# Running the mixer front in four groups of 1, 2, 3 and 2 blocks instead of three of 1, 3 and 4, beside the expert retrieval

## The reference, cut to what matters

```
n  = rmsnorm(x) * (1 + sc1) + sh1
z  = n @ w_in                          # 1024 x 4096, split in a_lin, a_gate, u, v, g_a, g_b
a  = a_lin * sigmoid(a_gate)
a  = silu(layernorm(causal_dwconv(hist ++ a, width 31))) @ w_conv_out     # branch A
v  = layernorm(v)
b  = (u * (tril(w_s) @ v + b_s)) @ w_gmlp_out                             # branch B, chunks of 128
m  = sigmoid(g_a) * a + sigmoid(g_b) * b
x  = x + gt1 * (m @ w_out)
n2 = rmsnorm(x) * (1 + sc2) + sh2
q  = n2 @ w_q;  s1, s2 = q halves @ keys; top 16 of each; top 16 of their 16 x 16 sums -> 128 experts a token
act = gelu(u_tab[eid] . n2);  x = x + gt2 * sum(softmax * act * v_tab[eid])
y  = rmsnorm(x)
```

## Time and profile before

| | us |
|---|---|
| median of three runs | 3551.34 (3548.37 to 3553.54) |
| the profiled execution | 3556.78 |
| its span | 3555.2 |
| first gather | 275.3 |
| first gather of block 1 | 923.5 |
| first gather of block 4 | 2154.6 |
| first gather of block 5 | 2478.5 |
| busy: TensorE, VectorE, ScalarE, GpSimd | 2051.7, 2448.6, 441.8, 1249.4 |

### The profile page before, as it was taken

One profiled execution on the slowest core, in us unless ns is written; L12 is line 12 of the kernel. 1 busy time (PEld: TensorE's weight loads), 2 busy tenths in 40 slices (PEclk: granted clock), 3 DMA queues, 4 the chain that ended last, 5 costly groups with the idle time before them and its releaser, 6 DMA issues. The chain is left out here.

```text
span 3555.2 us, 28830 instructions
## 1 busy us (share of the span) xinstructions
PE 2051.7 (58%) x9548; PEld 995.9 (28%) x9548; DVE 2448.6 (69%) x6290; ACT 441.8 (12%) x1031; POOL 1249.4 (35%) x1046
## 2 busy tenths in 40 slices
PE   6873878986277777778688623333343333355333
PEld 4762444643144344455345300000000000000000
DVE  1447574479898796655768997766866697656665
ACT  1121101011111110110211011101010101011100
POOL 0001221222233433333434334544454444445343
PEclk9886988998588888899799855555555555555555
DMA  7734756798579999899999869999999998998998
GB/s 297 311 144 166 301 207 260 272 358 318 220 283 360 363 334 371 329 383 419 395 410 406 345 251 401 375 422 422 368 417 421 422 386 354 421 421 341 423 421 343
DMA packets 183925, 1232.08 MB, mean 347 GB/s; under 512 B 30512, under 2 KB 31152, under 8 KB 36320
## 3 DMA queue, kind: packets, MB, share of 16 engines
q0 software_dynamic: 148608, 1082.20, 75.9%
q1 hardware_dynamic: 35168, 148.05, 10.6%
HBM read 1221.14 MB, written 9.02 MB: 346 GB/s over the span
## 5 line engine op out<-in xcount | busy, mean ns | idle before, releaser
L1045 POOL DMA_INDIRECT big<-in_experts,eid x920 | 1112.0, 1209 | 2081.9 <-PE ps L765 1620.4
L1507 DVE SCALAR_TENSOR_TENSOR big<-big,xr 128x1024 f32<-128x1024 f32 x920 | 1113.6, 1225 | 525.3 <-DMA big<-in_experts,eid 520.2
L765 PE MATMUL ps<-big,wd 128*32 128x512 f32 x3680 | 726.2, 873 | 1089.8 <-DVE wd L1524 1085.2
L530 PE MATMUL ps<-big,wring 128*128 128x260 f32 (+2 forms) x2400 | 644.9, 423 | 81.5 <-issue 56.3
L530 PEld LDWEIGHTS ps<-big,wring 128*128 128x128 f32 x2400 | 447.6, 201 | 318.7 <-issue 166.1
L765 PEld LDWEIGHTS ps<-big,wd 128*32 128x32 f32 x3680 | 85.0, 127 | 1591.0 <-DVE wd L1524 1535.7
L987 ACT ACTIVATE gel<-act 128x2 f32<-128x2 f32 x516 | 105.7, 205 | 2569.9 <-DVE big L1507 2322.8
L1524 DVE TENSOR_SCALAR wd<-mask,gel,gate 128x32 f32<-128x32 f32 x1024 | 275.1, 363 | 152.3 <-ACT gel L987 141.5
L765 PE MATMUL ps<-w,wd 128*32 128x512 f32 x208 | 100.3, 1061 | 174.7 <-DVE wd L1524 170.8
L1205 DVE SCALAR_TENSOR_TENSOR arena<-arena,wdw 128x128 f32<-128x128 f32 (+2 forms) x360 | 182.9, 572 | 0.0
L682 PE MATMUL ps<-wring,mbuf 128*128 128x256 f32 (+1 forms) x528 | 128.6, 400 | 11.6 <-DMA wring<-in_w_out 6.3
(11 more groups left out here) (219 smaller groups left out, 1881.0 us busy)
## 6 DMA issues: line engine op xcount, KB each, us to landing
wring<-in_w_in SPq DMA_DIRECT2D x40, 1024.0 KB
wring<-in_w_q SPq DMA_DIRECT2D x19, 1024.0 KB
big<-in_experts,eid POOLq DMA_INDIRECT x920
wring<-in_w_ada SPq DMA_DIRECT2D x12, 1024.0 KB
wring<-in_w_out SPq DMA_DIRECT2D x9, 1024.0 KB
big<-in_w_ada SPq DMA_DIRECT2D x6, 1024.0 KB, 6.9
xr<-in_w_ada SPq DMA_DIRECT2D x6, 1024.0 KB, 8.8
big<-in_w_in SPq DMA_DIRECT2D x4, 1024.0 KB, 14.7
```

The costliest lines, as they stand in the source:

```text
L530: mm = mmul(out, piece(n)[:, c, col:col + P], src[:, c, gi * tg:(gi + 1) * tg], start=(c == 0), stop=(c == k - 1))
L765: mm = mmul(ps[QUAD * j:QUAD * (j + 1), half, :], wd[:, 2 * (at % 4) + jj, :], row(2 * slot + jj)[:, D + 512 * h:D + 512 * (h + 1)], start ...
L1045: gp.indirect_dma_start(row(r), None, t["experts"], bass.IndirectOffsetOnAxis(ap=index, axis=0)).then_inc(s_row[r], 16)
L1507: last = v.scalar_tensor_tensor(out=row(r)[:, 0:D], in0=row(r)[:, 0:D], scalar=1.0, in1=x, op0=ALU.mult, op1=ALU.mult, accum_out=act[:, c: ...
```

## The change

There are four groups: block 0; blocks 1 and 2; blocks 3, 4 and 5; blocks 6, 7 and the samples. Each has `ng` = 1, with `tg` = 128, 256, 384 and 264. The fronts of the last three are dealt out over pairs 0 to 60, 64 to 188, and 204 to 312 (`FRONT_AT`). `WIDE_AT`, the pair from which five pair buffers serve, moves from 4 x 64 to 5 x 64. The later routings move too (`routing`): one turn of the second group at pair 64, two of the third at 192 and 202, the samples' at 320 and block 7's at 384. All groups now share one set of semaphores, with `base` the sum over the groups ahead. The tiles of the arena are as wide as the widest group (384), and x for the third group is loaded early into `xn1`, which has six blocks instead of four. The four waits ahead of the last group's x refer to the third group.

```diff
-NB1 = 4
+STARTS = [0, 1, 3, 6]
+NB1 = STARTS[-1]
+NBL = NBT - NB1
+SB = NBL - 1
+GT = (NBL - 1) * P + NS
+GX = 3 * P
 GW = 520
+AGAIN = 4
+LAST = len(STARTS)
...
-END_B = 60
-END_C = 4 * PAIRS - 8
-WIDE_AT = 4 * PAIRS
+FRONT_AT = {2: (0, PAIRS - 4), 3: (PAIRS, 3 * PAIRS - 4), 4: (3 * PAIRS + 12, 5 * PAIRS - 8)}
+WIDE_AT = 5 * PAIRS
...
-        S = {f"{n}{g}": ctx.enter_context(nc.semaphore(f"{n}{g}")) for n in group_names for g in (1, 2)}
+        S = {n: ctx.enter_context(nc.semaphore(n)) for n in group_names}
...
-            g.base = totals(G1) if n == 2 else {}
-
-            g.order = list(range(g.nb)) if n < 3 else [0, 1, 2, 4, 3]
+            g.base = {}
+            for ahead in GROUPS:
+                g.base = {k: g.base.get(k, 0) + v for k, v in totals(ahead).items()}
+
+            g.order = list(range(g.nb)) if n < LAST else [*range(SB - 1), SB, SB - 1]
...
-        G1 = group(1, [0], P, xn1[:, 0:1, :], mbuf)
-        G2 = group(2, [1, 2, 3], 3 * P, xn1[:, 1:4, :], mbuf)
-        G3 = group(3, list(range(NB1, NBT)), 260, xn2, wring)
+        GROUPS = []
+        for n in range(1, LAST):
+            blocks = list(range(STARTS[n - 1], STARTS[n]))
+            GROUPS.append(group(n, blocks, len(blocks) * P, xn1[:, blocks[0]:blocks[-1] + 1, :], mbuf))
+        GROUPS.append(group(LAST, list(range(NB1, NBT)), GT, xn2, wring))
...
-            for g, lo, hi in ((G2, 0, END_B), (G3, PAIRS, END_C)):
+            for g in GROUPS[1:]:
+                lo, hi = FRONT_AT[g.n]
...
+        routing = [(PAIRS, ROUTE_PIECES, G2, 1), (3 * PAIRS, ROUTE_PIECES, G3, 1),
+                   (3 * PAIRS + ROUTE_PIECES, ROUTE_PIECES, G3, 2), (5 * PAIRS, ROUTE_PIECES + 1, G4, 1),
+                   (6 * PAIRS, ROUTE_PIECES, G4, 2)]
...
-            for n in range(first_piece[2], first_piece[3] + 3):
+            for n in range(first_piece[2], first_piece[3]):
+                if n == first_piece[2] + 4:
+                    for b in G3.blocks:
+                        sp.dma_start(xn1[:, b, :], t["x"][b * P:(b + 1) * P, :]).then_inc(S["x_in3"], 16)
                 with_spill(n, G2)
-
-            sp.wait_ge(*G2.to("oa_mm", KC * G2.ng))
-            sp.wait_ge(*G2.to("s_done", NCH))
-            sp.wait_ge(*G2.to("sq_act", 1))
-            sp.wait_ge(*G2.to("tables", 1))
-            for b in G3.blocks:
+            for n in range(first_piece[3], first_piece[4] + 3):
+                with_spill(n, G3)
+
+            sp.wait_ge(*G3.to("oa_mm", KC * G3.ng))
+            sp.wait_ge(*G3.to("s_done", NCH))
+            sp.wait_ge(*G3.to("sq_act", 1))
+            sp.wait_ge(*G3.to("tables", 1))
+            for b in G4.blocks:
...
-            def routing_2():
-                for i in (1, 2):
-                    yield from route(G2, i)
-
-            def routing_3():
-                for i in range(1, 4):
-                    yield from route(G3, i)
-                yield from to_slots()
-                yield from route(G3, 4)
+            def later_routes():
+                for _, _, g, turn in routing:
+                    yield from route(g, turn)
+                    if g.blocks[g.order[turn]] == NB:
+                        yield from to_slots()
```

More of the change, by code:

```diff
@@ L367, in build @@
         front_steps = spread_front()
[L368 removed]
+        last_step = {n: hi - 1 for n, (_, hi) in FRONT_AT.items()}
         def beside_peer(begin, finish, fronts, extra, share=0.0):
@@ L454, in _ @@
             first_wo = max(n for n, p in enumerate(pieces) if p[0] == "wo") - 3
-            for n in range(first_piece[3] + 3, len(pieces)):
-                if n == first_piece[3] + 11:
-                    sp.wait_ge(*G3.to("a_done", CC * G3.ng))
-                    sp.dma_start(t["out_hist_p"], aT[:, :, AW - W + 1:AW]).then_inc(S["out_hist"], 16)
+            for n in range(first_piece[4] + 3, len(pieces)):
+                if n == first_piece[4] + 11:
+                    sp.wait_ge(*G4.to("a_done", CC * G4.ng))
+                    sp.dma_start(t["out_hist_p"], aT[:, :, G4.np:G4.np + W - 1]).then_inc(S["out_hist"], 16)
@@ L786, in begin @@
                         made[0] += 1
-            beside_peer(begin, value, {2: front(G2), 3: front(G3)}, lambda at: None, share=0.5)
+            beside_peer(begin, value, {g.n: front(g) for g in GROUPS[1:]}, lambda at: None, share=0.5)
         @block.scalar
@@ L826, in norm @@
                         w = width(b)
-                        x = (x_first if g.n == 3 and turn == 0 else g.xn)[0:w, i, :]
+                        x = (x_first if g.n == LAST and turn == 0 else g.xn)[0:w, i, :]
                         out = sq_a[0:w, i, :] if g.n == 1 else part(big, 6 * 2 * D, 4, D)[0:w, i % 4, :]
@@ L966, in front @@
                     ac(gts, bank2(6)[0:NS, :], ACT.Copy).then_inc(s["gt_done"], 1)
-                yield from gap(27 if g.n == 3 else 11)
+                yield from gap(19 if g.n == LAST else 11)
                 next(g.numerators)
@@ L1001, in root @@
                 ac(stat[:, 1, lo:hi], stat[:, 0, lo:hi], ACT.Sqrt).then_inc(S["fin_root"], 1)
-            exps = {PAIRS + ROUTE_PIECES * i + 6: G2 for i in range(2)}
-            exps |= {at + 6: G3 for at in (4 * PAIRS, 5 * PAIRS, 6 * PAIRS, 6 * PAIRS + ROUTE_PIECES + 1)}
+            exps = {start + 6: g for start, _, g, _ in routing}
             copies = {half_start(h - 1) + 20 + c: (h, c) for h in range(2, 2 * NB) for c in range(8)}
@@ L1017, in extra @@
                     root(1, 0, NB)
-            beside_peer(gelu, lambda at: None, {2: front(G2), 3: front(G3)}, extra)
+            beside_peer(gelu, lambda at: None, {g.n: front(g) for g in GROUPS[1:]}, extra)
             square(NB)
@@ L1595, in to_slots @@
                 yield
-            def routing_2():
-                for i in (1, 2):
-                    yield from route(G2, i)
-            def routing_3():
-                for i in range(1, 4):
-                    yield from route(G3, i)
-                yield from to_slots()
-                yield from route(G3, 4)
-            second, third, norms = routing_2(), routing_3(), early_norm()
-            def extra(at):
-                if PAIRS <= at < PAIRS + 2 * ROUTE_PIECES:
-                    next(second, None)
-                for b, count in ((4, ROUTE_PIECES), (5, ROUTE_PIECES), (6, 2 * ROUTE_PIECES + 1)):
-                    if b * PAIRS <= at < b * PAIRS + count:
-                        next(third, None)
+            def later_routes():
[3 more added lines that the diff above has]
+                        yield from to_slots()
+            routes, norms = later_routes(), early_norm()
+            def extra(at):
+                for start, count, _, _ in routing:
+                    if start <= at < start + count:
+                        next(routes, None)
                 if at - 2 in ends:
@@ L1619, in _ @@
             dve.wait_ge(S["mask_made"], 1)
-            beside_peer(dots, weigh, {2: front(G2), 3: front(G3)}, extra)
+            beside_peer(dots, weigh, {g.n: front(g) for g in GROUPS[1:]}, extra)
             take_acc(2 * NB)
```

123 lines of the change are left out of this document (62 added, 61 removed).

## The result

The changed kernel takes 3641.1 us (3638.0 to 3648.7, four runs) against 3550.3 on the same chips, 91 us slower. The ratio on record is 1.0271, 95% interval 1.025 to 1.0291; the two medians by themselves give 1.0256, inside it. The forecast was 3580 us, 29 slower; the range ended at 3640. The direction was right, the size a third of what came, and the range was missed by 1 us.

A forecast was written before the change was run, and what follows sets the result against it. It took transfers to bound the second half and TensorE most first-stage stretches. First stage -115, middle and block 4 +164, blocks 5 to 7 -20 sum to +29 us on 3551.3: 3580 us, range 3505 to 3640.

The forecast's parts named there:

- What it adds: Whole kernel: 33.6 MB of weights read again, wide products unchanged, taps and semaphores costing nothing, narrow buffering 0.2 us a pair.
- First stage: Block 0's 64 pairs, with two blocks' front beside them instead of three: 115 us less, bounds 140 and 90.
- The 25 us that I had given back: First stage's five TensorE stretches: 13 us for query transfers and 12 for DMA and stalls, leaving 88 of 113 saved.
- Middle and block 4: Pairs 64 to 320, third and fourth fronts and the pairs after them: 1719 us against 1555.0, 164 more.
- Bytes at 415 GB/s plus gaps: Middle and block 4: each time split into transfers at 415 GB/s and a gap; added weights 81 us, gaps 47.
- Bounds: Middle and block 4: 1653 to 1793 us by narrow or wide gaps; all terms' extremes -62 to +143 us.
- Blocks 5 to 7: Blocks 5 to 7 and the samples: about one routing turn each in blocks 5 and 6, 20 us less (5 to 25).
- (a): Front stretches: time follows TensorE's and VectorE's busy time together, not bytes and gaps; 23 us less, 3528; chance 0.28.
- (b): Fronts: each group keeps the old gaps, its chains having as many steps whatever its width; +118 us, 3669; chance 0.15.
- (d): Fourth front: TensorE's clock at the lower level makes it the bound, 59 us over the term; 3639; chance 0.07.
- (c): Whole kernel: the terms cancel and no change can be told, 3551 us; chance 0.12.
- two signs of being wrong: Middle and block 4 under 1690 us, weights hidden in gaps; or first stage above 560 us, set by the pairs.

The follow-up runs named there:

- the run with short taps: Changed kernel with the fourth group's convolution taps working on 8 columns instead of 256: 1.026 of the kernel before.
- the query hand-over: Changed kernel with TensorE and ScalarE two steps later in the query stretch: 1.0187 of the kernel before, 30 us less than the changed kernel.
- SP's order: Changed kernel with SP issuing, in the branches, the next w_in piece before the next branch output piece: 1.0213 of the kernel before, 21 us less than the changed kernel.
- the spread front: Changed kernel with the fourth front over pairs 204 to 376 instead of 312, five buffers from 384, last two routings at 384 and 395: 1.0191 of the kernel before.

## Why the prediction was right in direction and wrong in size

**What it adds.** Right: bytes (+32.5 MB), as many wide products, taps at nothing (the run with short taps). Semaphores were put at nothing too, which no run tested. Narrow buffering was put at 0.2 us a pair, 13 us; alone it is 16.

**First stage.** Predicted 115 less, measured 91.6. The 25 us that I had given back in the five stretches were 52 (they fell by 61 and not by 88). With an eighth of the group's bytes the stage is 530 us, so about half of the 52 is bytes and the waits for them. Some 15 are TensorE's busy time, which fell by 98 and not by 113; how the shares overlap is open. That term was mis-sized. Two others missed and nearly cancelled: the time between the listed stretches fell by 41 where 21 were expected, and the tail, put at 2 less, is 17 longer, with 20 gathers in it instead of 11. The start fell by 7, put at 4. (The five stretches of the earlier trace rows hold 80 gathers, not 83; that changes about 1 us.)

**Middle and block 4.** Predicted 1719 us, measured 1761. This is the step that failed most, in its gaps. These stretches of the changed kernel hold the same work as the first, third and fourth of the earlier trace rows (start with a and gate columns; the two branches with mean and variance; w_out with the queries), three of the third front, then three of the fourth:

```profile
830.70:984.80 154.10, 107.36 (x392) 47.28 (x392) 122.51 (x307) 18.41 (x46) 52.17 (x44) 0.79 0.86 338
1066.30:1302.00 235.70, 180.59 (x656) 84.39 (x656) 150.06 (x297) 28.14 (x64) 67.04 (x62) 0.86 0.82 315
1302.00:1628.20 326.20, 234.72 (x1016) 122.48 (x1016) 225.24 (x712) 34.95 (x88) 121.25 (x104) 0.83 0.96 386
1813.60:1937.80 124.20, 76.27 (x336) 45.81 (x336) 92.26 (x210) 18.27 (x38) 36.23 (x30) 0.76 0.75 294
2009.40:2203.10 193.70, 136.15 (x616) 85.89 (x616) 124.38 (x272) 26.45 (x61) 63.28 (x54) 0.83 0.89 345
2203.10:2473.00 269.90, 193.45 (x932) 114.01 (x936) 181.49 (x543) 34.24 (x97) 102.28 (x86) 0.83 0.96 389
```

By the prediction's own measure, time times (1 - GB/s / 415), the gaps are 29, 57 and 23 us where it had 33, 32 and 7, and 36, 33 and 17 where it had 24, 22 and 4. With the rest of each front, which came near its terms, they add up to 145 and 137; the prediction had 120 and 104. So the excess lies mainly in the stretches with the branches and in those with w_out and the queries. The prediction had scaled these gaps down from the old large group, which has 5 steps to a half head, by the number of blocks; groups of 3 steps have a wait that it hardly has (37 and 34 us for VectorE's search against 4).

Told by pairs instead, without the 34 and 41 us of the tails, which mostly fall behind pairs 188 and 312, the fronts were put at 801 and 700 and the stretches after them at 136 and 82. Measured: 832 and 734, then 127 and 68. So the fronts are 31 and 34 too long, what follows 9 and 14 too short. The third front's excess is the query hand-over (22 us by that run's stretch, 831.9 to 810.0) and the waits for weights (7, by the run with SP's order, 824.7). In the fourth front the same are 6 and 7, and some 21 us are not assigned to a step; density may be in them. The branch stretches alone have 25 and 11 us more gap than predicted and SP's order gave back 7 in each front, so what else holds them is not shown.

**The form of the sum.** "Bytes at 415 GB/s plus gaps" was the deeper error. It priced the 33.6 MB at 81 us; the fourth front gives back 35 for 29.4 MB. It was luck that the sum missed by no more: bytes priced some 40 us too high and gaps put some 60 us too low work against each other.

**Bounds.** Those of this term are mis-added: by its own terms they are 1650 and 1785, not 1653 and 1793, and the upper extreme of the range would be 135 us slower, not 143.

**Bandwidth rule.** The Trainium skill, DMA: Bandwidth & Descriptors, section Bandwidth, has about 358 GB/s for transfers from HBM, a core's share while both cores of the domain stream. The rows after, with one core at work, show 408 over 1019 us, and 415 in a front's query stretch; here it doesn't bind.

**Blocks 5 to 7.** Predicted 20 less, measured 21.9. The parts were not as stated: block 5 took 319.5 us and block 6 340.5, where 331 each were expected.

**Rivals.** (a), time after TensorE's and VectorE's busy time together, gave 864 and 692 for the fronts, measured 832 and 734, and 501 for the first stage, measured 557. It fell, and the taps show that VectorE's time doesn't count everywhere. (b), +118 (110 with its sum put right), is nearest in size (+91) and nearest in the gaps, 150 and 140 where 145 and 137 came. Its reason, chains with as many steps whatever the group's width, doesn't hold as it stands: the query hand-over is a wait that the old large group hardly had, and the spread front shows that the price is not fixed. (d): TensorE was granted 0.78 in the fourth front, not the lower level, so it did not happen. (c) fell. Neither of the two signs of being wrong that the prediction named came: the middle with block 4 was not under 1690 us, and the first stage, at 556.6, stayed just under 560. It failed by a third way that it had not named.

## What to carry to other kernels

Where several engines walk through one order of steps with a fixed lag, changing how many steps a unit of work has can turn a wait that was always fulfilled into one for work that the other engine does in the same step or later; count the steps of both sides before changing a group's shape. Reading the weights once more cost between 0.4 and 0.7 of bytes over bandwidth beside gathers that nearly filled the DMA engines, and the gap grew when the bytes went; don't add bytes and gaps as if they were apart. Splitting the work in smaller groups is only half a change: the fourth front alone, dealt out over 172 pairs instead of 108, gave back a third of the loss.

## What the runs showed of the hardware

With most of the query hand-over gone, TensorE's granted clock in the third group's query stretch rose from 0.86 to 0.94. Its busy time there fell from 142.9 to 132.5 us, for 576 and 568 matmuls; the 8 that are missing are one pair's value products, some 1 us. The two levels are 1.2 and 2.4 GHz. In the stretch with the lower mean TensorE was idle 42 of 185 us, nine of its waits being for VectorE's search, up to 7.2 us long; in the other it was idle 31 of 163, with two such waits; 16 shorter ones, up to 4.2 us, were for the pairs' `weigh`. The Trainium skill, TensorE: Matmul & The Clock Gate, section What's actually happening, has the lower level follow idleness; the rows agree.
